# A streaming encoder layer with hierarchical experts: the fifth expert's weights are loaded after the first two gathers

## The reference, cut to what matters

```
h = rms_norm(x)
group = argmax(h @ w_group)                        # 4 groups
top2  = two best of the 8 experts in that group    # logits h @ w_erouter
for e in range(32):
    ye = (silu(h @ w_gate[e]) * (h @ w_up[e])) @ w_down[e]
    y += combine[:, e] * ye
```

## Time and profile before

| | us |
|---|---|
| median of the runs before | 699.75 |
| the profiled execution, its own time | 700.71 |
| its span, first to last instruction | 699.0 |
| TensorE busy | 574.2 (82%) |
| VectorE busy | 238.6 (34%) |
| ScalarE busy | 193.5 (28%) |
| GpSimd busy | 87.0 (12%) |

### The profile page before, as it was taken

The page is one execution under the profiler, slowest core; times in us unless marked ns, Lnnn a source line. Parts: engine busy times, 40 slices in busy tenths (PEclk is TensorE's granted clock), DMA queues, the critical chain, the costliest instruction groups (busy, mean ns, idle before and its releaser), DMA issues.

```text
span 699.0 us, 8352 instructions
## 1 busy us (share of the span) xinstructions
PE 574.2 (82%) x3356; PEld 379.3 (54%) x3356; DVE 238.6 (34%) x497; ACT 193.5 (28%) x440; POOL 87.0 (12%) x123
## 2 busy tenths in 40 slices
PE   5999997999999688887998926999968787878830
PEld 4878785777787466664787823444323333333310
DVE  3730333667264255555424471101100000000107
ACT  4450452434141454355423430111111111111110
POOL 4000000013720500002000011111211111110010
PEclk9999998999999879898999956999988999999985
DMA  8111130212338810006838895899999999999539
GB/s 298 64 62 60 61 120 1 68 54 76 122 127 342 317 49 1 1 1 241 360 123 328 323 402 178 359 416 429 425 423 424 426 423 424 424 427 424 222 134 362
DMA packets 24248, 166.41 MB, mean 238 GB/s; under 512 B 4704, under 2 KB 5232, under 8 KB 11024
## 3 DMA queue, kind: packets, MB, share of 16 engines
q1 hardware_dynamic: 17168, 146.31, 52.0%
q0 software_dynamic: 6320, 16.92, 6.3%
q10 hardware_dynamic: 720, 2.62, 0.9%
HBM read 154.69 MB, written 17.43 MB: 246 GB/s over the span
## 4 chain that ended last, share of the span: by engine, by line
PE 59%; DMA 24%; DVE 9%; ACT 4%; issue 3%; SPq 1%; POOLq 0%; ACTq 0%; DVEq 0%
DMA egu<-in_w_gu 18%; PE twin L2058 11%; PE twin L1619 8%; PE twin L1620 8%; PE twin L1621 8%; PE twin L2078 3%; PE twin L1863 3%; PE twin L1864 2%; PE twin L1865 2%; DMA yg<-ye_dram 2%; PE twin L1999 1%; PE twin L1933 1%; DVE xsT L1555 1%; DMA X<-in_x 1%; DMA Kc<-in_cache_kt 1%
## 5 line engine op out<-in xcount | busy, mean ns | idle before, releaser
L2058 PE MATMUL twin<-egu,xsT 128*64 128x512 f32 x512 | 128.7, 660 | 38.4 <-DMA egu<-in_w_gu 32.6
L2058 PEld LDWEIGHTS twin<-egu,xsT 128*64 128x64 f32 x512 | 46.3, 150 | 110.6 <-issue 110.6
L1619 PE MATMUL twin<-wH,hH 128*128 128x512 f32 x240 | 98.8, 412 | 0.0
L1620 PE MATMUL twin<-wL,hH 128*128 128x512 f32 x240 | 95.7, 399 | 0.0
L1621 PE MATMUL twin<-wH,hL 128*128 128x512 f32 x240 | 95.4, 397 | 0.0
L1561 DVE TENSOR_TENSOR hs<-sil,twin 128x256 f32<-128x256 f32 x16 | 6.7, 422 | 163.5 <-ACT sil L1004 163.5
L2078 PE MATMUL twin<-edn,hTs 128*64 128x512 f32 x256 | 58.1, 592 | 1.1 <-ACT hTs L1008 1.1
L1004 ACT ACTIVATE sil<-twin 128x256 f32<-128x256 f32 x16 | 6.1, 384 | 178.2 <-PE twin L2058 178.2
L1068 DVE SCALAR_TENSOR_TENSOR wL<-win,colt,wH 128x512 fp32r<-128x512 f32 x48 | 33.3, 755 | 60.0 <-ACT wH L731 60.0
L1619 PEld LDWEIGHTS twin<-wH,hH 128*128 128x128 f32 x240 | 46.3, 193 | 11.1 <-issue 2.1
L1621 PEld LDWEIGHTS twin<-wH,hL 128*128 128x128 f32 x240 | 46.3, 193 | 10.2
(11 more groups left out here) (304 smaller groups left out, 764.3 us busy)
## 6 DMA issues: line engine op xcount, KB each, us to landing
egu<-in_w_gu SPq DMA_DIRECT2D x32, 2048.0 KB, 35.2
edn<-in_w_dn SPq DMA_DIRECT2D x32, 1024.0 KB, 39.3
win<-in_w_main SPq DMA_DIRECT2D x12, 1024.0 KB, 5.2
Kc<-in_cache_kt SPq DMA_DIRECT2D x8, 1024.0 KB, 8.5
Vc<-in_cache_v SPq DMA_DIRECT2D x8, 1024.0 KB, 7.0
X<-in_x SPq DMA_DIRECT2D x10, 512.0 KB, 9.2
yg<-ye_dram SPq DMA_DIRECT2D x5, 1024.0 KB, 8.9
win<-in_w_out SPq DMA_DIRECT2D x4, 1024.0 KB, 6.2
```

Of the source, the lines that this page charges most:

```text
L1619: pe.matmul(bank[i][:, :], hH[:, d, i, :], wH[k][:, cs], start=(d == 0), stop=False)
L1620: pe.matmul(bank[i][:, :], hH[:, d, i, :], wL[k][:, cs], start=False, stop=False)
L2058: ins = pe.matmul(bank[2 + q][CAP * j:CAP * j + CAP, :], xsT[q][:, c, j * CAP:(j + 1) * CAP], egu[places[j]][:, c, :], start=(c == 0), sto ...
```

## The change

On SP, the two loads of expert 4 leave the place where they were issued with those of expert 3, and come after the wait for the first two gathers. The gate and up part comes ahead of that of expert 5, and the down part after it. No load is added or removed, and no other engine's program is changed.

```diff
             sp.wait_ge(out_done, 4 * NT)
-            for e in (3, 4):
-                gate_up_of(e)
-                down_of(e)
+            gate_up_of(3)
+            down_of(3)
 
             for k in range(NXS):
                 sp.wait_ge(gath[k], 16)
+            gate_up_of(4)
             gate_up_of(5)
+            down_of(4)
             for e in range(NBUF, NE + 2, 2):
                 if e < NE:
                     sp.wait_ge(gu_done, e // 2 - 2)
```

## The result

The changed kernel took 705.58 us as the median of 20 runs (702.15 to 709.85); the kernel before, in as many runs beside them, 702.55 us (698.66 to 704.72). The ratio is 1.0048 with a 95% interval of 1.0028 to 1.0068, that is 3.4 us slower (2.0 to 4.8). This is inside 1%, and slower beyond the measurement's uncertainty. The 699.75 us that the forecast started from were the median of three runs, low among the twenty; so the predicted 705.0 us lie nearer to the measured 705.58 than the shift behind them does: 5.2 us were forecast, 3.4 measured.

A forecast was written before the change was run, and what follows sets the result against it. The prediction took the full weight stream on the DMA engines as the bound: 7.4 us for the moved bytes, less what a hole takes back, left 5.2 us. On the median 699.75 this gave 705.0 us, range 701.0 to 707.6.

The forecast's parts named there:

- What bounds the kernel: Weight stream on the DMA engines, full from 440 to 650 us at 424 GB/s; bytes still owed are paid at the end.
- the last product: Gate and up product of the last pair on TensorE; 1.7 us more if slow, not added.
- the hole: Near-idle DMA time behind expert 5's load, 437 to 439 us, which expert 4's loads would fill: 2 us.
- The whole price: Expert 4's two loads, 3.146 MB at 424 GB/s, moved behind 428.84: 7.4 us of the whole DMA.
- What is given back: Part of the 7.4 us absorbed behind the gathers, where only expert 5's load was ready; 5.2 us left to pay.
- mean over the DMA engines: Bound from 428 to 446 us: 1.41 MB more carried, 1.74 MB or 4.1 us still owed.
- last engine: Bound by the latest DMA engine: only 437 to 439 is free on every engine, leaving 5.4 us.
- The covers: Claims that pair 2's weights, SP's queue, GpSimd's third gather and the last pair's product add nothing to the cost.
- All paid: Rival: the slowest DMA engine has no real pause, so 7.4 us are paid, 707.2 us or 708.9; chance 0.16.
- Gathers sooner: Rival: stores land sooner, so GpSimd's gathers start earlier; a few tenths, 704.5 us; chance of a gain 0.03.
- Slack: Rival: bytes do not set the end, so the change is free, 699.8 us; chance 0.11 together with no move.
- No move: Rival: the gathers' wait on SP ends long before 428.84, so loads hardly move; chance 0.11 together with slack.

The follow-up runs named there:

- the doses: Edits to SP's loads of experts 3, 4 or 5, putting off or bringing forward -1.05 to 6.29 MB against the kernel before; stretches 224.16 to 238.24 us.
- the second dose: Against the changed kernel, expert 3's loads also wait for the gathers, a further 3.146 MB put off: 714.03 us, ratio 1.0162 to the kernel before.

## Why the prediction was right, point by point

**What bounds the kernel** was right. The stream's rate from 440 to 650 did not change, and the doses moved the start of the last product by their bytes, less what the hole took up. TensorE's own speed did not: where pair 14's product took 7.09 us in place of 8.78, the last one waited 4.15 us in place of 2.44, so that both sums are 11.2 us.

**The whole price, 7.4 us**, was right: the second dose cost 7.5 us.

**What is given back** is the term that was sized too low: 2.2 us forecast, 3.4 measured. The prediction had bounds of 4.1 us (mean over the DMA engines) and 5.4 us (last engine) for what is left to pay, and took 5.2; the traces measured 4.0. The step that failed is the one that counted the hole as the 2 us in which the DMA engines do nothing. The hole takes up 3.4 us, because its edges count too: from 436.84 to 440.84 the kernel before moved 122 GB/s and the changed kernel in the same place 425. That is (425 - 122) x 4 us = 1.2 MB, 2.9 us, and the rest, (340 - 301) x 8 us = 0.3 MB or 0.7 us, comes out of the first 8 us behind the issue; 3.6 us by this count, 3.4 by the stretch. The mean over bytes, which counts the edges, was the right one, but not in its parts: it left the first 8 us as they were and gave the rest 1.41 MB, where 1.2 MB were gained. The experiments did not follow single DMA engines, so why the late landing of expert 5's load (9.8 us) did not cost more is open; they show only that the pause could be filled.

**The covers** held. Pair 2 did not wait for weights; SP's later issues delayed nothing; GpSimd's third gather cost nothing that is seen in the stretch. The last product was named as a possible 1.7 us more, not added: it was 8.54 us in one trace of the changed kernel and 7.09 in the other, so leaving it out of the sum was right for the change, though a single run can have it: from the last product's start to the span's end the traces with 7.09 us have 43.2 to 43.8 us, the others 44.7 to 45.3.

**The rivals.** All paid: its condition, a pause of under 0.4 us on the slowest engine, is refuted by the 2.5 us that the down part of expert 5 gained there. The prediction's own argument against it has a slip: a mean share of 0.03 of 16 engines over two microseconds is 0.03 x 16 x 2 = 0.96 us of work if one engine did all of it, not half a microsecond; a pause of 1.0 us would still have been left. The Trainium skill's rule to issue a DMA early ("DMA: Bandwidth & Descriptors", "Rules for kernel authors") has the right sign for the change. The later issue cost 4.0 us; the full 7.4 us that the prediction read into the rule are seen only in the second dose, and an earlier issue into the full stream gained nothing (230.67 against 230.69 us). Gathers sooner: the wait for the stores did become shorter, and the wait for the indices grew by as much, to 8.05 us in the changed kernel and 12.50 without the loads of experts 3 and 4; the 17.07 to 17.11 us from the router to the first gather leave no room for it. Slack: refuted by every dose over 2 MB. No move: refuted by SP's rows, 429.98 in place of 400.83.

**The sum.** 5.2 us forecast, 4.0 us by the traces, 3.4 us (2.0 to 4.8) by the times. Both lie under the 4.1 to 6.5 us that the prediction gave the forecast itself; the 6.5 is worked out from no row. The predicted 705.0 us fit the measured 705.58 better than that, because the level of three runs, 699.75, stood 2.8 us under that of twenty; that part was luck. So was the start of the last product, 660.7 by the prediction and 660.67 in the first trace: 4.07 us of it come from the change, and 1.14 us from the time ahead of the issue, which varies by itself. The 1% that the prediction took for what a measurement of this kernel can just tell was too much: twenty runs told 0.48% from no change.

## What to carry to other kernels

When a queue of transfers is full up to the end, price a moved load by the bytes still owed when the queue becomes gapless, with the rate of its full stretch, and take the bytes of the partly filled stretches into account, not their empty microseconds alone. Then look at the last hole: a load whose place is already free and that stands behind a wait can go into it, as the down part of expert 5 did for 0.38% (0.11 to 0.66). Where the times of single runs spread by more than the effect, compare a stretch between two events of the trace that holds the change alone; here it repeated to 0.3 us, while the times spread over 6 us.

## What was not expected of the hardware

A pause of two microseconds in the DMA traffic was worth 3.4 us, since the run-down before it and the run-up behind it move less too (122 GB/s over the four microseconds around it). And the last product's length, 7.09 or 8.5 to 8.8 us, changed from trace to trace of one kernel. Its granted clock goes with it: 1.00 throughout in the kernel before, 0.50 for the first 3 us in the first trace of the changed kernel, and 0.50 for 3 us from its second microsecond on in the second dose.

```profile
655.46:662.55 7.09, 7.09 (x34) 2.96 (x36) 0.00 (x0) 0.00 (x0) 0.00 (x0) 1.00 0.30 123
```

```profile
660.67:663.67 3.00, 3.00 (x8) 1.08 (x10) 0.00 (x0) 0.00 (x0) 0.00 (x0) 0.50 0.32 134
```

```profile
668.00:671.20 3.20, 3.20 (x10) 1.22 (x8) 0.00 (x0) 0.00 (x0) 0.00 (x0) 0.50 0.30 125
```

In the three traces in which TensorE had waited 4.15 or 4.16 us the clock fell to 0.50 for part of the product. In the five in which it had waited 2.44 to 2.47 us it did not fall; in the second dose, after 2.50 us, it fell 1.3 us into the product. These runs do not settle when it falls.
